# The product of odds and remaining stick, moved from VectorE to GpSimd in the prompt's stick-breaking stage

## The reference, cut to what matters

```python
def stick_breaking_block(q, q_pos, k, v, k_pos, sb_bias):
    z = jnp.einsum('bqhd,blhd->bhql', q, k).astype(jnp.float32) * (HEAD_DIM ** -0.5)
    z = z + sb_bias.astype(jnp.float32)[None, :, None, None]
    mask = (k_pos[None, :] < q_pos[:, None])[None, None]
    log_1m = jnp.where(mask, jax.nn.log_sigmoid(-z), 0.0)
    suffix = lax.cumsum(log_1m, axis=3, reverse=True) - log_1m
    a = jnp.where(mask, jnp.exp(jax.nn.log_sigmoid(z) + suffix), 0.0)
    o = jnp.einsum('bhql,blhd->bqhd', a.astype(v.dtype), v)
```

## Time and profile before

| | |
|---|---|
| time, median of 3 runs | 2425.16 us (2413.54, 2425.16, 2425.19) |
| the profiled execution's own time | 2416.84 us |
| its span in the trace | 2415.3 us |
| PE busy | 2012.3 us, 83% of the span |
| DVE busy | 960.5 us, 40% |
| ACT busy | 587.1 us, 24% |
| POOL busy | 106.3 us, 4% |

### The profile page before, as it was taken

How to read it: one execution, slowest core, us unless ns; L and a number is a source line. 1 busy time by engine, 2 the same in 40 slices (tenths; PEclk the granted TensorE clock), 3 DMA queues, 4 the chain that set the end, 5 groups by cost and what they waited for, 6 DMA issues and landing times. The chain is left out here.

```text
span 2415.3 us, 31463 instructions
## 1 busy us (share of the span) xinstructions
PE 2012.3 (83%) x11374; PEld 1658.5 (69%) x11374; DVE 960.5 (40%) x1750; ACT 587.1 (24%) x929; POOL 106.3 (4%) x192
## 2 busy tenths in 40 slices
PE   2799999997777638775984869399999999999984
PEld 2677889995444425543442857299999999999973
DVE  3344000101628625442111621444545555555544
ACT  3110111214737513321111110331222121222112
POOL 0000000001101013320000000000000000000000
PEclk8899999998778759997997989599999999999997
DMA  2845543115624059974151430121011111011102
GB/s 100 304 147 196 200 157 143 47 46 147 146 75 167 1 196 343 343 269 182 64 227 74 147 144 1 53 65 48 18 52 52 52 35 43 26 52 52 35 9 90
DMA packets 131723, 274.45 MB, mean 114 GB/s; under 512 B 23081, under 2 KB 74618, under 8 KB 128634
## 3 DMA queue, kind: packets, MB, share of 16 engines
q1 hardware_dynamic: 111962, 164.95, 19.9%
q0 software_dynamic: 19680, 108.42, 12.8%
HBM read 243.91 MB, written 79.10 MB: 134 GB/s over the span
## 5 line engine op out<-in xcount | busy, mean ns | idle before, releaser
L451 PE MATMUL ff_ups<-act_hi,ff_up_hi 128*128 128x364 f32 (+1 forms) x1056 | 233.5, 330 | 14.9 <-DVE ff_up_lo L1813 14.9
L451 PE MATMUL ff_ups<-act_lo,ff_up_hi 128*128 128x364 f32 (+1 forms) x1056 | 233.3, 329 | 0.0
L451 PE MATMUL ff_ups<-act_hi,ff_up_lo 128*128 128x364 f32 (+1 forms) x1056 | 233.2, 329 | 0.0
L1864 DVE TENSOR_TENSOR act_x<-act_x,ff_dps 128x512 f32<-128x512 f32 (+1 forms) x198 | 135.9, 686 | 215.4 <-PE ff_dps L1915 215.4
L451 PEld LDWEIGHTS ff_ups<-act_hi,ff_up_hi 128*128 128x128 f32 x1056 | 183.8, 188 | 16.5 <-DVE ff_up_lo L1813 15.0
L426 PE MATMUL inp_ps<-inp_w_hi,h_hi 128*128 (+1 forms) x432 | 169.3, 392 | 22.5 <-DVE inp_w_lo L385 20.7
L451 PEld LDWEIGHTS ff_ups<-act_hi,ff_up_lo 128*128 128x128 f32 x1056 | 183.5, 188 | 0.0
L451 PEld LDWEIGHTS ff_ups<-act_lo,ff_up_hi 128*128 128x128 f32 x1056 | 183.5, 188 | 0.0
L426 PE MATMUL inp_ps<-inp_w_lo,h_hi 128*128 (+1 forms) x432 | 169.0, 391 | 0.0
L426 PE MATMUL inp_ps<-inp_w_hi,h_lo 128*128 (+1 forms) x432 | 168.6, 390 | 0.0
L1915 PE MATMUL ff_dps<-ff_dn_hi,ff_f_hi 128*128 128x512 f32 (+1 forms) x396 | 157.8, 398 | 9.3 <-DVE ff_f_lo L1854 9.3
(11 more groups left out here) (248 smaller groups left out, 3292.9 us busy)
## 6 DMA issues: line engine op xcount, KB each, us to landing
ss_pages<-in_pool POOLq DMA_DIRECT2D x128, 256.0 KB, 4.8
ss_pages<-in_pool SPq DMA_DIRECT2D x128, 256.0 KB, 4.6
out_s<-in_cache POOLq DMA_DIRECT2D x8, 4080.0 KB, 20.6
ff_up_raw<-in_w_up SPq DMA_DIRECT2D x44, 512.0 KB, 5.0
inp_raw<-in_w_in POOLq DMA_DIRECT2D x10, 2048.0 KB, 9.7
sd_kv<-in_cache SPq DMA_DIRECT2D x8, 2048.0 KB, 19.5
zs<-inp_zt SPq DMA_DIRECT2D x48, 256.0 KB, 4.4
ff_dn_raw<-in_w_down SPq DMA_DIRECT2D x22, 512.0 KB, 4.4
```

The source lines that it names most:

```text
L451: last = pe.matmul(out[:, n * 512:n * 512 + b - a], lhs, rhs[:, a:b], start=(i == 0), stop=(i == len(pairs) - 1))
L1864: dve.tensor_tensor(x, x, dps[0:n, k * 512:k * 512 + 512], ALU.add).then_inc(added, 1)
```

## The change

The 32 products leave DVE's queue and stand in POOL's, behind the 16 copies. Operands, widths, buffers, the wait for `left_done` and the count on `a_done` stay as they are; no other queue is edited.

```diff
             for t in range(QT):
                 pool.wait_ge(row_in[t], 16)
             extra_pool(pool)
+            for n in range(2 * N):
+                L = length(n // 2)
+                pool.wait_ge(left_done, n + 1)
+                pool.tensor_tensor(odds[:, n % 8, 0:L], odds[:, n % 8, 0:L], suffix[:, n % 4, 0:L], ALU.mult).then_inc(a_done, 1)
...
-            def weigh(n):
-                L = length(n // 2)
-                dve.wait_ge(left_done, n + 1)
-                dve.tensor_tensor(odds[:, n % 8, 0:L], odds[:, n % 8, 0:L], suffix[:, n % 4, 0:L], ALU.mult).then_inc(a_done, 1)
-
...
             for it in range(-2, N + 2):
-                for h in range(2):
-                    if 0 <= it < N:
-                        weigh(2 * it + h)
                 if it + 2 < N:
                     exponents(it + 2)
```

## The result

The changed kernel takes 2431.27 us in the median of 14 runs (2424.16 to 2436.17); the kernel before, beside it, 2423.45 us (14 runs, 2413.54 to 2429.42). The ratio is 1.0027, with a 95% interval of 1.0016 to 1.0039: 6.5 us slower, between 3.9 and 9.4. That is small, within the 0.5% that the prediction calls "same", and clear of zero. (The two medians alone lie 7.8 us apart, inside that interval.) The profiled execution took 2426.53 us with a span of 2425.0. It is the second fastest of its 14, and the profiled execution of before (2416.84) also lies 6.6 us under its median, so neither trace shows a typical execution of its kernel.

The account below looks back on a forecast made before the run. The prediction took TensorE to bound the kernel, and a chain of waits round several engines this stage. A loss of 5.3 us less 0.7 gained made +4.6 on a base of 2421.0, forecast 2426 us, range 2414 to 2440.

Parts of the forecast that it names:

- What bounds the stage: Over the whole stage: no engine is full; a chain of waits round several engines bounds it, and the product lies beside it.
- The ring: In each iteration: scan, leave, odds, weight copies, soften, next scan; claimed not to wait for the product of its own iteration.
- Relief of 0.7 us: Early scans on DVE: time gained by removing products, 0.40 us at the scan at 752 plus 0.3 us for five others.
- five more early scans: Scans from 727 to 758 us with gaps of 0.1 us or none; taken to gain 0.3 us together.
- The stall of 5.3 us: At PE's first weights: the first products wait behind POOL's 16 copies until 730.76 us, delaying everything once by 5.3 us.
- The product's own cost: On POOL: each product taken at the scan's rate, 406 ns at 128 columns to 2278 at 1024, 43 us in total.
- 3.6 us of cover: At the stage's end: last product done near 836.8 us, PE wants it at 840.45, so the end costs nothing.
- (1): At the first products: POOL not free at 730.76 us, products start only when copies have landed; +22.4 us, 2443 us; chance 0.09.
- (2): Where a pair's first product overlaps its second scan: scan and product slow each other; +15 us, 2436 us; chance 0.07.
- (3): Early half, products up to 512 columns: DVE was the bound, 7.7 us gained; sum -2.4 us, 2419 us; chance 0.14.
- (4): Whole stage: DVE was the bound throughout, 24.0 us gained; sum -18.7 us, 2402 us; chance 0.03.
- The sum: Over the kernel: 5.3 us lost less 0.7 us gained is +4.6 us, giving 2426 us, 0.2% above, called "same".

Follow-up runs that it names:

- interleaved kernels: Changed kernel with each of the 16 copies behind one of the first 16 products, not all ahead of the first; timed twice, 1.0000 and 0.9996 of before.
- the doubled products: Changed kernel with every product made twice on GpSimd, the first into a tile nobody reads; timed 1.0065 (1.0051 to 1.0080).

## Why the prediction was right, point by point

*What bounds the stage.* Right. The ring of scan, leave, odds, weight copies and soften kept its 12.59 us when the product left DVE (12.2 to 12.6 over the profiles looked at, with the product on either engine), and saved time turned into idle time. I expected about 24 us of it ahead of the scans; without the stall it is 16, and 15 in the interleaved kernels (31.4 us against 16.3). The rest of the saved 22.8 stands ahead of other work of DVE.

*Relief of 0.7 us.* The one term that can be read alone: from the seventh scan to the eighth it takes 5.35 us instead of 5.68 (43.75 to 49.10 against 36.72 to 42.40 us from the stage's start), 0.33 for my 0.40 (and 5.36 on POOL against 5.68 on DVE in the two kernels with copies last). The 0.3 us for five more early scans did not show: in those two, the seventh scan starts 42.39 us into the stage with products on POOL and 42.40 on DVE. In the kernels with the copies out of the way the timing shows no gain, 1.000 and 0.9996; 0.7 us is below what it can tell.

*The stall of 5.3 us.* Right in place and mechanism, and in size at the first weights. First products at 730.73 for 730.76 forecast, first weights 5.06 us later against the stage's start. "The whole 5.3 us shift through" was too much: what it costs in the end is 3.9 us at equal clock, since one microsecond returns where the clock rises, which the prediction left out. Spreading the copies removes the stall, and with it the change's whole loss in the timing (1.0027 to 1.0000 and 0.9996).

*The product's own cost.* I took 2.28 us at 1024 columns; it is 2.31 to 2.35 alone and 2.75 in the mean, as the first of each pair waits for a scan. At 128 columns 0.46 for 0.41. The total is 49 us for 43, and all but the start is hidden, as said. The last products end at 843.08 and PE takes them at 846.19; I gave 3.6 us of cover, it is 3.1.

*The rivals.* (1) did not occur: the first product starts 0.11 us after the last copy's issue ends at 730.62. The 6 us for the first call of a freshly loaded routine (the Trainium skill, GPSIMD Engine Reference, Instruction dispatch) do not occur here, the first product taking 0.47 us; so no such load shows in this trace. (2) did not occur in the changed kernel, scans being 2279 ns for 2278, because the scan is always there first; the doubled products show the same mechanism at work when it is not. (3) gave the early half 7.7 us; up to the ninth pair the kernel with products on POOL gains 0.32 us on the one on DVE (53.63 against 53.95 us into the stage, both with copies last). (4) is out by the ring's unchanged length.

*The sum.* +4.6 us forecast; 5.3 in the stage by the first profiles, 3.9 to 9.4 by the timing. That the first profiles agree so well with the forecast is luck: the rise comes after 17 us in one and after 33 in the other, and the second profiles differ by 10.5 us (136.2 and 146.7). What carries the forecast is the place of the stall, its 5 us at the first weights and the timings with and without it. The margin between 4.6 and 6.5 is not resolved: the clock can move the stage by as much, and I gave it plus or minus 2 us where the same kernel shows 5 between two profiles. Of the 5 us by which the time forecast (2426 us) fell short of 2431.27, 2.4 lie in the base that I took, 2421.0 where the kernel before had 2423.45 beside the change.

## What to carry to other kernels

Moving work to an idle engine costs what stands ahead of it in that engine's queue, once, and that can be more than all that the move gains; look at the first use, not at the average. An operation that lies beside the ring of waits gave next to nothing when it left a busy engine, and nothing was lost by its running over twice as long elsewhere, as long as it did not hold up the scans. Where profiles of a stage differ by a few us, compare them at equal clock history before a cause is named. Time shows what one profile can't: the interleaved kernels had a longer stage in their profiles than the change and no loss in their timings. And try giving TensorE something to do in the wait ahead of a stage: here that gained about as much (7.6 us) as the change under study lost.

## What the runs showed of the hardware that I had not expected

- The rise of TensorE's clock in this stage came 17 to 40 us after its beginning over all kernels, 0 to 8 us apart in two profiles of one kernel, and the stage of the change was 5 us of 140 longer with the later one. Fourteen products in TensorE's idle time brought the rise forward to 716.5 us in the profile, 3.3 us into the stage, and that kernel gained 0.31% (0.21 to 0.42).
- A semaphore increment on GpSimd behind 16 DMA issues was seen 1.0 us before the last issue ended (one run), while the first product started 0.11 us after it.
- Scan (VectorE) and product (GpSimd), both with two SBUF inputs, hold each other up: the product lost 0.8 us of the 1.0 us that it lay under a scan that came first, and with GpSimd's products in hand the scans of 640 columns took 2206 ns in the mean instead of 1480.
- Behind 16 copies of 10 MB in all, a store of 1024 KB landed after 25.4 us instead of 4.0.
